# A three-layer block on one core: last chunk's taps on two engines, scores between taps, transposes by pairs of heads, low part and variance moved

## The chip, the cores and the metric

The kernel runs on one core of a Trainium2 chip. The metric is the device time of one launch in microseconds; three runs took 1165.66, 1166.23 and 1166.40 us, median 1166.23. The engines are named as in the profile: TensorE (PE, its weight loads PEld), VectorE (DVE), ScalarE (ACT), GpSimd (POOL) and SyncE (SP), which issues nearly all DMAs.

## The reference

Input x has 256 tokens of 1024 features in float32. Two layers of a first kind are followed by one of a second kind. Cut to what matters here:

```python
# layers 0 and 1: attention over chosen keys beside a gated recurrence, then a gated FFN
h = rmsnorm(x, norm_mix[l]); proj = h @ w_in[l]          # q, k, v, index, recurrence, gates
y_attn = dsa_attention(q, k, v, qi, ki, wi)              # softmax over the 64 keys of the highest index score
y_hgrn = rmsnorm(hgrn2_chunked(q_h, k_in, v_h, log_f)) * silu(hg)
x = x + (sigmoid(ga) * (y_attn @ w_proj_attn[l]) + sigmoid(gb) * (y_hgrn @ w_proj_hgrn[l])) @ w_out[l]
g, u = split(rmsnorm(x, norm_ffn[l]) @ w_ffn_in[l]); x = x + (silu(g) * u) @ w_ffn_out[l]

# third layer: attention with forgetting beside a causal depthwise convolution
attn = fox_attention(q, k, v, log_f)                     # 8 heads of 64, two blocks of 128 queries
u = conv_val * sigmoid(conv_gate)
u = causal_depthwise_conv(u, conv_w, conv_b)             # 31 taps, 512 channels
u = silu(layer_norm(u, conv_ln_g, conv_ln_b))            # mean and variance over the 512 channels
y = concatenate([attn, u]) @ w_o
x = x + g1 * rms_norm(y, mix_post_g); h = rms_norm(x, ffn_pre_g) * (1 + sc2) + sh2
x = x + g2 * rms_norm(swiglu_ffn(h), ffn_post_g)
```

## The kernel before

All activations lie in SBUF with features on the 128 partitions and 256 tokens along the free axis, a chunk being 128 features. Weights stream through in units of at most 128x2048 elements. SP loads each into one of six raw buffers; ACT rounds it to a high part (w_hi, all of ACT stands under L1066), DVE subtracts to get the low part (w_lo, L1609), and TensorE forms three products, high by high, high by low and low by high. Both parts have three buffers, so a unit is split up to three units ahead, once TensorE has finished the unit that held the buffer (unit_done). The order of work is written out by hand, engine by engine: `stream(n)` on TensorE does the next n units, `tick` and `split_ahead` on ACT and DVE split one more, and semaphores (an `Event` each) tie the engines. Parts that several engines share are written as generators: each `next(first)` or `next(second)` takes the attention of the first or second 128 queries one step further, `next(taps)` the last chunk of the convolution.

Attention on TensorE (`attend`, L722): scores for eight heads, then, when ACT's exponentials are done (event a_ex, one for all heads of a query tile), transposes of the probabilities (8 for the first tile, 16 for the second) into four banks that ACT copies out, the products with v, and four transposes of the result, of which ACT makes the high part and DVE the low part (ya_lo, event a_lo). In layers 0 and 1 the recurrence's first products (L958) wait for a_lo of the second tile. DVE makes that low part at L2016, after the decayed queries (L2013), the first block products and a reversed identity.

The convolution of the third layer has four chunks of 128 channels. DVE does chunks 0 to 2 tap by tap (`conv`, L2180), each tap adding one shifted product to an accumulator (conv_acc); over two chunks the operations alternate, over one each waits for the one before. The last chunk is on TensorE (`last_chunk`, L788): 31 matmuls of 256 columns, each with a diagonal of that tap's weights that ACT has made (`diagonals`, L1512), eight per step of the generator; ACT copies the sum and adds the bias (L1569). DVE then folds the four chunks (L2245 to L2250, event c_fold), TensorE sums over the channels (L1041), ACT scales the mean, DVE centres (L2255), ACT squares, DVE folds the squares (c_fold2), TensorE sums them (the variance, L1046), and ACT makes the factor (Ln, Exp), silu and the high parts, and then eight diagonals of gains (`diagonal_gains`), which `gain_rows(0)` (L802) needs. The output projection is four units (L540 to L542 with ya_hi, then conv_out_hi); `gain_rows(0)` stands behind the second, `gain_rows(1)` behind the fourth. Then rows are normed token by token (`mixer_out`, L1185) and transposed back (L825), and the feed-forward's first unit (`high_parts_first`, L830) starts with the high parts alone.

## Time and profile before

| | us |
|---|---|
| median of three runs | 1166.23 |
| lowest, highest | 1165.66, 1166.40 |
| the profiled execution | 1165.65 |
| its span | 1163.9 |
| TensorE busy | 1128.3 (97%) |
| VectorE busy | 857.0 (74%) |
| ScalarE busy | 628.4 (54%) |
| chain that ended last | PE 73%, DVE 17%, ACT 7%, issue 2%, DMA 1% |

The first layer fills the span up to about 420 us, the second up to about 832, the third the rest. Inside the third, the attention and the convolution lie between 896 and 938, the output projection between 937.6 and 961.3. Times in the rows are microseconds from the span's start. A row of the timeline may hold several like instructions (x8); its second number then runs from the first one's start to the last one's end. A matmul's time includes a tail of some 0.2 us that overlaps the next one, so the pace is read from starts. fp32 operands make two records for each tap's matmul. In brackets stands how long the engine was idle before the group, and what released it. Some records of TensorE are missing.

### The profile page before, as it was taken

What the parts mean: (1) busy time and instruction counts of PE and PEld (TensorE: products, weight loads), DVE (VectorE), ACT (ScalarE), POOL (GpSimd) and SP (SyncE); (2) the same over time, 40 slices, a digit from 0 to 9 for tenths busy, and PEclk for the clock granted to TensorE, in tenths of its full rate; (3) what the DMA queues carried; (4) which work ended last, traced back from release to release, by engine and by line L of the source; (5) the groups of instructions that cost most, each with busy time, mean ns of one, the idle gap of its engine ahead of it and who ended that gap; (6) DMA issues with size and microseconds to landing.
All of it is one profiled execution on the core that took longest, in us unless ns stands there. A gap on an engine that the chain in (4) does not pass through costs nothing.

```text
span 1163.9 us, 20299 instructions
## 1 busy us (share of the span) xinstructions
PE 1128.3 (97%) x8518; PEld 1081.5 (93%) x8518; DVE 857.0 (74%) x1348; ACT 628.4 (54%) x802; POOL 0.2 (0%) x4
## 2 busy tenths in 40 slices
PE   6999999999999999999999999999999998999997
PEld 5899899999999998898999999999998888999997
DVE  7896676777889878975767778898689857445544
ACT  6676366464443466673574644344578586434333
POOL 0000000000000000000000000000000000000000
PEclk9999999999999999999999999999999999999999
DMA  9645443756879555554336668796544044565520
GB/s 345 205 145 184 140 136 120 249 185 227 278 250 311 177 166 171 164 184 140 117 113 227 204 205 281 243 322 208 172 140 169 21 155 143 190 192 188 181 73 37
DMA packets 174027, 214.09 MB, mean 184 GB/s; under 512 B 3696, under 2 KB 155632, under 8 KB 173936
## 3 DMA queue, kind: packets, MB, share of 16 engines
q1 hardware_dynamic: 173248, 212.14, 55.6%
q8 instruction: 67, 1.10, 0.4%
q10 hardware_dynamic: 688, 0.66, 0.2%
q14 instruction: 24, 0.20, 0.1%
HBM read 211.74 MB, written 1.05 MB: 183 GB/s over the span
## 4 chain that ended last, share of the span: by engine, by line
PE 73%; DVE 17%; ACT 7%; issue 2%; DMA 1%; DVEq 0%; ACTq 0%
PE stream L540 15%; PE stream L542 15%; PE stream L541 15%; DVE w_lo L1609 7%; PE steps L540 5%; PE steps L541 5%; PE steps L542 5%; ACT w_hi L1066 3%; ACT probs L1066 2%; DVE conv_acc L2190 2%; PE stream L798 1%; PE steps L974 1%; PE steps L777 1%; DVE probs L1801 1%; PE stream L624 1%
## 5 line engine op out<-in xcount | busy, mean ns | idle before, releaser
L1609 DVE TENSOR_TENSOR w_lo<-raw,w_hi 128x2048 fp32r<-128x2048 f32 (+2 forms) x178 | 401.6, 2266 | 187.0 <-ACT w_hi L1066 186.2
L1066 ACT ACTIVATE w_hi<-raw 128x2048 fp32r<-128x2048 f32 (+2 forms) x178 | 336.2, 1892 | 298.1 <-PE stream L542 258.4
L540 PE MATMUL stream<-h_hi,w_hi 128*128 128x256 f32 x1592 | 455.4, 286 | 3.2 <-DVE w_lo L1609 2.8
L541 PE MATMUL stream<-h_lo,w_hi 128*128 128x256 f32 x1592 | 450.4, 283 | 0.0
L542 PE MATMUL stream<-h_hi,w_lo 128*128 128x256 f32 x1592 | 450.3, 283 | 0.0
L540 PEld LDWEIGHTS stream<-h_hi,w_hi 128*128 128x128 f32 x1592 | 305.3, 192 | 7.2 <-DVE w_lo L1609 4.9
L541 PEld LDWEIGHTS stream<-h_lo,w_hi 128*128 128x128 f32 x1592 | 305.4, 192 | 1.4 <-issue 1.0
L542 PEld LDWEIGHTS stream<-h_hi,w_lo 128*128 128x128 f32 x1592 | 305.3, 192 | 0.0
L540 PE MATMUL steps<-gu_hi,w_hi 128*128 128x256 f32 x352 | 100.0, 284 | 0.2 <-DVE gu_lo L1912 0.2
L541 PE MATMUL steps<-gu_lo,w_hi 128*128 128x256 f32 x352 | 99.6, 283 | 0.0
L542 PE MATMUL steps<-gu_hi,w_lo 128*128 128x256 f32 x352 | 99.6, 283 | 0.0
L1880 DVE SCALAR_TENSOR_TENSOR ada_sum<-ada_raw,c_act,ada_sum 128x256 f32<-128x256 f32 x168 | 81.5, 485 | 6.0
L1066 ACT ACTIVATE gu_hi<-gu 128x512 fp32r<-128x512 f32 x33 | 20.9, 632 | 101.6 <-DVE gu L1908 101.6
L540 PEld LDWEIGHTS steps<-gu_hi,w_hi 128*128 128x128 f32 x352 | 67.5, 192 | 0.6 <-issue 0.4
L541 PEld LDWEIGHTS steps<-gu_lo,w_hi 128*128 128x128 f32 x352 | 67.5, 192 | 0.0
L542 PEld LDWEIGHTS steps<-gu_hi,w_lo 128*128 128x128 f32 x352 | 67.5, 192 | 0.0
L624 PE MATMUL stream<-w_hi,h_hi 128*128 128x512 f32 (+1 forms) x152 | 59.5, 391 | 1.4 <-DVE w_lo L1609 1.4
L626 PE MATMUL stream<-w_lo,h_hi 128*128 128x512 f32 (+1 forms) x152 | 58.1, 382 | 0.0
L625 PE MATMUL stream<-w_hi,h_lo 128*128 128x512 f32 (+1 forms) x152 | 57.9, 381 | 0.0
L1912 DVE TENSOR_TENSOR gu_lo<-gu,gu_hi 128x512 fp32r<-128x512 f32 x33 | 22.9, 693 | 23.1 <-ACT gu_hi L1066 23.1
L2190 DVE SCALAR_TENSOR_TENSOR conv_acc<-conv_in,params,conv_acc 128x256 f32<-128x256 f32 x90 | 38.9, 481 | 1.0
L540 PE MATMUL stream<-x_gained_hi,w_hi 128*128 128x256 f32 x128 | 36.8, 287 | 1.0 <-DVE x_gained_lo L1663 1.0
(370 smaller groups left out, 1641.9 us busy)
## 6 DMA issues: line engine op xcount, KB each, us to landing
raw<-in_w_ffn_in SPq DMA_DIRECT2D x66, 1024.0 KB, 5.5
raw<-in_w_in SPq DMA_DIRECT2D x54, 1024.0 KB, 5.3
raw<-in_w_ffn_out SPq DMA_DIRECT2D x33, 1024.0 KB, 5.1
ada_raw<-in_ada_w SPq DMA_DIRECT2D x24, 1024.0 KB, 6.4
raw<-in_w_out SPq DMA_DIRECT2D x8, 1024.0 KB, 5.1
raw<-in_w_proj_attn SPq DMA_DIRECT2D x8, 512.0 KB, 3.5
raw<-in_w_proj_hgrn SPq DMA_DIRECT2D x8, 512.0 KB, 4.5
raw<-in_w_o SPq DMA_DIRECT2D x4, 1024.0 KB, 5.2
```

The costliest lines, as they stand in the source:

```text
L540: pe.matmul(dst, w_h, x_h, start=start, stop=False, skip_group_check=True)
L541: pe.matmul(dst, w_h, x_l, start=False, stop=False, skip_group_check=True)
L542: return pe.matmul(dst, w_l, x_h, start=False, stop=stop, skip_group_check=True)
L624: pe.matmul(dst, h_h[:, k0 + k, ts], hi[:, k, :], start=k0 + k == 0, stop=False)
L625: pe.matmul(dst, h_l[:, k0 + k, ts], hi[:, k, :], start=False, stop=False)
L626: mm = pe.matmul(dst, h_h[:, k0 + k, ts], lo[:, k, :], start=False, stop=k0 + k == KC - 1)
L777: mm = pe.matmul(pv[:, DH * h:DH * h + DH], prT[:, h, s, :], v[:, s, DH * h:DH * h + DH], start=s == 0, stop=s == qt)
L1066: return act.activation(out_, in_, func, **kw)
L1609: tt(wl[m % SPL][:, 0:n], raw[m % RAW][:, 0:n], wh[m % SPL][:, 0:n].bitcast(F32), ALU.subtract)\
L1880: ins = stt(acc, w[:, k, :], cact[:, k:k + 1], acc, ALU.mult, ALU.add)
L1912: tt(gu_l[i % 2].rearrange("p c t -> p (c t)"), gu, gu_h[i % 2].rearrange("p c t -> p (c t)").bitcast(F32), ALU.subtract).then_inc(*lane.m ...
L2190: ins = stt(cv[:, c, :], src, w, cv[:, c, :], ALU.mult, ALU.add)
```

## The change

Seven edits. (1) The last chunk has 23 taps on TensorE; the other eight are on DVE, alternating with the last eight of chunk 2, the first of them with the bias. DVE adds TensorE's sum to them (c_tap, one operation); ACT's copy and eight of its diagonals go. (2) TensorE's taps come in portions of 4, 4 and 15 instead of 8, 8, 8 and 7, with the second tile's scores behind the second portion, and DVE takes these scores ahead of taps 22 and on. (3) In all layers a_ex counts pairs of heads, and the transposes wait pair by pair. (4) In layers 0 and 1 the low part of the second tile stands ahead of the decayed queries. (5) The variance's matmul stands behind the first unit of the output projection, and the fold of the squares behind all of the attention's last steps on DVE; the mean's matmul comes after the products with v. (6) The first square of the updated rows (`x_squares(0)`) comes after the second row factor. (7) In the feed-forward's first unit the first two feature chunks are released one by one.

TensorE, third layer, from the second half of the scores to the projection; q_and_pick and k_and_cum are queries and keys with the decay, conv_diagonal the taps, probs the probabilities, h_norm_third the folded convolution, scratch its squares. Before:

```order
L736 MATMUL steps<-k_and_cum,q_and_pick 128x256 [waits ya_lo_set]
L736 MATMUL steps<-k_and_cum,q_and_pick 128x256 x3
L798 MATMUL stream<-conv_in,conv_diagonal_155 128x256 [waits diagonals_set]
...
L798 MATMUL stream<-conv_in,conv_diagonal_169 128x256
L746 MATMUL steps<-consts,probs 128x128 [waits probs_set]
L746 MATMUL steps<-consts,probs 128x128 x15
L1041 MATMUL stream<-h_norm_third,ones 128x256 [waits conv_folded]
L757 MATMUL steps<-v,probsT 128x64 [waits probsT_set]
...
L767 MATMUL steps<-consts,y_tm 128x128 [waits second_y_scaled]
...
L1046 MATMUL stream<-scratch,ones 128x256 [waits conv_squares_folded]
L767 MATMUL stream<-consts,y_tm 128x128 [waits second_y_scaled,evac_by_act]
...
L540 MATMUL steps<-w_hi_55,ya_hi 128x512 [waits ya_lo_set,second_ya_lo_set,evac_by_act,split_lo]
```

And now (L801 is the taps, L1047 the mean, L1053 the variance, L811 the gain rows):

```order
L738 MATMUL steps<-k_and_cum,q_and_pick 128x256 [waits ya_lo_set]
L738 MATMUL steps<-k_and_cum,q_and_pick 128x256 x3
L801 MATMUL stream<-conv_in,conv_diagonal_147 128x256 [waits diagonals_set]
...
L801 MATMUL stream<-conv_in,conv_diagonal_161 128x256
L749 MATMUL steps<-consts,probs 128x128 [waits probs_set]
L749 MATMUL steps<-consts,probs 128x128 x3
...
L760 MATMUL steps<-v,probsT 128x64 [waits probsT_set]
...
L1047 MATMUL stream<-h_norm_third,ones 128x256 [waits conv_folded]
L770 MATMUL steps<-consts,y_tm 128x128 [waits second_y_scaled]
...
L770 MATMUL stream<-consts,y_tm 128x128 [waits second_y_scaled,evac_by_act]
...
L542 MATMUL steps<-w_hi_55,ya_hi 128x512 [waits ya_lo_set,second_ya_lo_set,evac_by_act,split_lo]
...
L1053 MATMUL stream<-scratch,ones 128x256 [waits conv_squares_folded]
```

The scores moved ahead of the last fifteen taps, there are eight taps fewer, the transposes wait four times, the mean's matmul went behind the products with v, and the variance's matmul from between the last transposes to behind the first unit.

VectorE, third layer, from the first tile's low part to the mean's fold and centring. Before:

```order
L1835 TENSOR_TENSOR ya_lo<-steps,ya_hi 128x4x128 [waits ya_hi_set]
L2190 SCALAR_TENSOR_TENSOR conv_acc<-conv_in,params,conv_acc 128x256 [waits dve_lane] x4
L1801 ISA probs,row_max<-steps,consts 128x256 [waits logits]
...
L1807 TENSOR_SCALAR row_max<-row_max 128x8 [waits dve_lane]
L2190 SCALAR_TENSOR_TENSOR conv_acc<-conv_in,params,conv_acc 128x256 [waits dve_lane] x5
L1609 TENSOR_TENSOR w_lo_58<-raw_52,w_hi_55 128x2048 [waits unit_done,split_hi]
L2245 TENSOR_TENSOR h_norm_third<-conv_acc 128x256 [waits split_lo]
L2247 TENSOR_TENSOR h_norm_third<-h_norm_third,conv_acc 128x256 [waits dve_lane]
L2250 TENSOR_TENSOR h_norm_third<-h_norm_third,conv_acc 128x256 [waits last_chunk_set,dve_lane]
L1609 TENSOR_TENSOR w_lo_59<-raw_53,w_hi_56 128x2048 [waits unit_done,split_hi]
L2255 TENSOR_TENSOR conv_acc<-conv_acc,rstd 128x1024 [waits conv_mean]
```

And now:

```order
L1843 TENSOR_TENSOR ya_lo<-steps,ya_hi 128x4x128 [waits ya_hi_set]
L1809 ISA probs,row_max<-steps,consts 128x256 [waits logits]
...
L1815 TENSOR_SCALAR row_max<-row_max 128x8 [waits dve_lane]
L2199 SCALAR_TENSOR_TENSOR conv_acc<-conv_in,params,conv_acc 128x256 [waits dve_lane] x2
L2196 TENSOR_SCALAR conv_acc<-conv_in,params 128x256
L2199 SCALAR_TENSOR_TENSOR conv_acc<-conv_in,params,conv_acc 128x256 [waits dve_lane] x14
L1617 TENSOR_TENSOR w_lo_58<-raw_52,w_hi_55 128x2048 [waits unit_done,split_hi]
L2255 TENSOR_TENSOR h_norm_third<-conv_acc 128x256 [waits split_lo]
...
L2260 TENSOR_TENSOR conv_acc<-stream,conv_acc 128x256 [waits last_chunk_summed,dve_lane]
L2262 TENSOR_TENSOR h_norm_third<-h_norm_third,conv_acc 128x256 [waits dve_lane]
L1617 TENSOR_TENSOR w_lo_59<-raw_53,w_hi_56 128x2048 [waits unit_done,split_hi]
L2267 TENSOR_TENSOR conv_acc<-conv_acc,rstd 128x1024 [waits conv_mean]
```

The scores come directly behind ya_lo; behind them stand 17 taps' operations where there were five, and four additions where there were three.

VectorE, first layer, between the second tile's result and the recurrence. Before:

```order
L1609 TENSOR_TENSOR w_lo_59<-raw_50,w_hi_56 128x2048 [waits unit_done,split_hi]
L2013 TENSOR_TENSOR hgrn_q_decayed<-hgrn_q,scratch 128x512 [waits hgrn_q_set]
L2013 TENSOR_TENSOR hgrn_q_decayed<-hgrn_q,scratch 128x512
L1845 TENSOR_TENSOR block_forget_99<-scratch 128x512
L2015 TENSOR_TENSOR reversed_ident<-consts,ones 128x128
L1835 TENSOR_TENSOR ya_lo<-steps,ya_hi 128x4x128 [waits ya_hi_set]
```

And now:

```order
L1617 TENSOR_TENSOR w_lo_59<-raw_50,w_hi_56 128x2048 [waits unit_done,split_hi]
L1843 TENSOR_TENSOR ya_lo<-steps,ya_hi 128x4x128 [waits ya_hi_set,hgrn_q_set]
L2022 TENSOR_TENSOR hgrn_q_decayed<-hgrn_q,scratch 128x512 x2
L1853 TENSOR_TENSOR block_forget_99<-scratch 128x512
L2024 TENSOR_TENSOR reversed_ident<-consts,ones 128x128
L1617 TENSOR_TENSOR w_lo_60<-raw_51,w_hi_57 128x2048 [waits unit_done,split_hi]
```

ya_lo moved up over the two products, the block product and the reversed identity.

The diff, less renumbering and declarations:

```diff
@@ -739,9 +741,10 @@
                 if n % 2:
                     mm.then_inc(a_lg.sem, 1)
             yield
-            pe.wait_ge(*a_ex.at(b, qt))
             n_t = 0
             for h in range(H):
+                if h % 2 == 0:
+                    pe.wait_ge(*a_ex.at(b, 4 * qt + h // 2))
                 for s in range(qt + 1):
                     mm = pe.transpose(B[n_t // 4][:, P * (n_t % 4):P * (n_t % 4) + P], pr[:, h, P * s:P * s + P], ident)
                     n_t += 1
@@ -790,12 +793,12 @@
             for e, c in BANKS[UOUT[2] + 3][1]:
                 pe.wait_ge(evac[e], c)
             pe.wait_ge(*evacuated(unit(2, "val1")))
-            for j in range(CONV_K):
+            for j in range(CONV_PE):
+                if j in (4, 8):
+                    yield
                 if j % 8 == 0:
-                    if j:
-                        yield
                     pe.wait_ge(*c_diag.at(0, j // 8))
-                mm = pe.matmul(conv_bank[:, 0:T], diag[j], upad[:, 3, j:j + T], start=j == 0, stop=j == CONV_K - 1)
+                mm = pe.matmul(conv_bank[:, 0:T], diag[j], upad[:, 3, j:j + T], start=j == 0, stop=j == CONV_PE - 1)
             mm.then_inc(c_tap.sem, 1)
             yield
 
@@ -838,8 +841,11 @@
             lo = wl[m % SPL].rearrange("p (k n) -> p k n", k=KC)
             for j in range(4):
                 pairs = [(n, k) for n in range(2) for k in (2 * j, 2 * j + 1)]
-                pe.wait_ge(*n_hi.at(NTH_NORM[5], j))
-                for n, k in pairs:
+                if j:
+                    pe.wait_ge(*n_hi.at(NTH_NORM[5], j))
+                for k, n in ((k, n) for k in (2 * j, 2 * j + 1) for n in range(2)):
+                    if j == 0 and n == 0:
+                        pe.wait_ge(*(n_hi.at(NTH_NORM[5], 0) if k else h_first_hi.at(0)))
                     out, ws = bank(m)[:, T * n:T * n + T], (slice(None), k, slice(P * n, P * n + P))
                     pe.matmul(out, hi[ws], hh[:, k, :], start=k == 0 and n == 0, stop=False, skip_group_check=True)
                     pe.matmul(out, lo[ws], hh[:, k, :], start=False, stop=False, skip_group_check=True)
@@ -1035,18 +1041,18 @@
         next(taps)
         next(second)
         next(taps)
-        next(taps)
+        next(second)
         next(second)
         pe.wait_ge(*c_fold.at(0))
         mm = pe.matmul(conv_bank[:, T:2 * T], ones, hn2[:, 0, :], start=True, stop=True)
         mm.then_inc(c_ms.sem, 1)
         next(second)
         next(second)
+        stream(1)
         pe.wait_ge(*c_fold2.at(0))
         mm = pe.matmul(conv_bank[:, 0:T], ones, scr[:, 0, :], start=True, stop=True)
         mm.then_inc(c_var.sem, 1)
-        next(second)
-        stream(2)
+        stream(1)
         gain_rows(0)
         stream(2)
         gain_rows(1)
@@ -1188,10 +1194,9 @@
             out_squares(1, p_part.at(0, 1))
             out_factor(0)
             out_squares(2, p_part.at(0, 2))
-            x_squares(0)
             out_squares(3, (unit_done, UOUT[2] + 4))
             out_factor(1)
-            for j in range(1, 4):
+            for j in range(4):
                 x_squares(j)
             act.wait_ge(*x_ms2.at(0))
             f(rs_x, rest_x, ACT.Ln, scale=1.0 / D, bias=eps).then_inc(*lane.step())
@@ -1208,7 +1213,13 @@
                           bias=mod[:, 3, k:k + 1]).then_inc(*lane.step())
                     act.wait_ge(*lane.last)
                 else:
+                    if j == 0:
+                        act.wait_ge(*h_first.at(0))
+                        f(hh[:, 0, :], hn2[:, 0, :], ACT.Copy).then_inc(*lane.mark(h_first_hi))
                     act.wait_ge(*n_hn.at(NTH_NORM[5], j if j < 2 else 2))
+                    if j == 0:
+                        f(hh[:, 1, :], hn2[:, 1, :], ACT.Copy).then_inc(*lane.mark(n_hi))
+                        continue
                 f(hh[:, 2 * j:2 * j + 2, :], hn2[:, 2 * j:2 * j + 2, :], ACT.Copy).then_inc(*lane.mark(n_hi))
             rows_in(1)
 
@@ -1228,7 +1239,7 @@
                 scale = qsc[:, H * qt + h:H * qt + h + 1] if b < 2 else SCALE
                 ins = f(pr[:, h, 0:n_s], pr[:, h, 0:n_s], ACT.Exp, scale=scale, bias=mx[:, qt, h:h + 1],
                         accum_out=den[:, qt, h:h + 1])
-                if h == H - 1:
+                if h % 2:
                     ins.then_inc(*lane.mark(a_ex))
                 else:
                     ins.then_inc(*lane.step())
@@ -1561,12 +1572,9 @@
             f(v[:, :, UC * j:UC * j + UC], b2(here()), ACT.Copy).then_inc(*emptied())
             if j == 0:
                 next(first)
-                diagonals(3)
             split_ahead()
         next(first)
         next(second)
-        act.wait_ge(*c_tap.at(0))
-        f(cv[:, 3, :], conv_bank[:, 0:T], ACT.Identity, bias=pc("conv_b", 3)).then_inc(*lane.mark(c_pe))
         next(second)
         act.wait_ge(*gains_set.at(1))
         act.wait_ge(*c_ms.at(0))
@@ -2008,13 +2016,14 @@
             next(second)
             tick()
             dve.wait_ge(*q_act.at(b, 1))
+            next(second)
             for g in range(2):
                 gs = slice(2 * g, 2 * g + 2)
                 tt(qp[:, gs, :], hq[:, gs, :], scr[:, gs, :], ALU.mult).then_inc(*(lane.mark(r_m) if g else lane.step()))
             longer_blocks(0)
             tt(flip, ident[:, ::-1], ones, ALU.mult).then_inc(*lane.mark(flip_set))
-            next(second)
             tick()
+            dve.wait_ge(*flip_set.at(b))
             for t in range(NT):
                 dve.wait_ge(*r_lv.at(b, t))
                 tt(AT[:, :, t, :], A[t].rearrange("p (c q) -> p c q", c=RH),
@@ -2183,7 +2192,7 @@
                 for c in chunks:
                     o = COLS["conv_w"][0] + CONV_K * c + j
                     w, src = par[:, o:o + 1], upad[:, c, j:j + T]
-                    if j == 0:
+                    if j == (0 if c < 3 else CONV_PE):
                         ts_(cv[:, c, :], src, w, pc("conv_b", c), ALU.mult, ALU.add).then_inc(*lane.step())
                     else:
                         dve.wait_ge(lane.sem, lane.count + 1 - len(chunks))
@@ -2236,9 +2245,10 @@
         next(first)
         conv(range(18, 22), (2,))
         next(first)
-        conv(range(22, 26), (2,))
         next(second)
-        conv(range(26, CONV_K), (2,))
+        conv(range(22, CONV_PE), (2,))
+        dve.wait_ge(*lane.last)
+        conv(range(CONV_PE, CONV_K), (2, 3))
         step()
         split_ahead()
         dve.wait_ge(*lane.last)
@@ -2246,20 +2256,21 @@
         dve.wait_ge(*lane.last)
         tt(hn2[:, 0, :], hn2[:, 0, :], cv[:, 2, :], ALU.add).then_inc(*lane.step())
         dve.wait_ge(*lane.last)
-        dve.wait_ge(*c_pe.at(0))
+        dve.wait_ge(*c_tap.at(0))
+        tt(cv[:, 3, :], conv_bank[:, 0:T], cv[:, 3, :], ALU.add).then_inc(*lane.step())
+        dve.wait_ge(*lane.last)
         tt(hn2[:, 0, :], hn2[:, 0, :], cv[:, 3, :], ALU.add).then_inc(*lane.mark(c_fold))
         step()
         split_ahead()
         step()
         dve.wait_ge(*c_mu.at(0))
         tt(cv, cv, rs.unsqueeze(1).broadcast_to([P, 4, T]), ALU.subtract).then_inc(*lane.mark(c_cen))
-        next(second)
+        for _ in range(3):
+            next(second)
         dve.wait_ge(*c_sq.at(0))
         tt(scr[:, 0:2, :], scr[:, 0:2, :], scr[:, 2:4, :], ALU.add).then_inc(*lane.step())
         dve.wait_ge(*lane.last)
         tt(scr[:, 0, :], scr[:, 0, :], scr[:, 1, :], ALU.add).then_inc(*lane.mark(c_fold2))
-        next(second)
-        next(second)
         split_ahead()
         dve.wait_ge(*c_rs.at(0))
         for c in range(4):
```

## Rows read from the trace of the kernel before

**Rows 1.** The page: busy times, share of the span and instructions.
```profile
PE 1128.3 (97%) x8518; PEld 1081.5 (93%) x8518; DVE 857.0 (74%) x1348; ACT 628.4 (54%) x802; POOL 0.2 (0%) x4
```

**Rows 2.** Timeline of TensorE: start us, us, instruction group, idle time before and its releaser.
```profile
80.49 1.09 PE L746 MATMUL steps<-consts,probs 128*128 128x128 f32 x8 [1.04 <-ACT probs L1066]
...
81.34 0.36 PE L540 MATMUL stream<-h_hi,w_hi 128*128 128x256 f32 x1
...
110.28 1.97 PE L746 MATMUL steps<-consts,probs 128*128 128x128 f32 x16 [1.15 <-ACT probs L1066]
...
134.16 2.02 PE L958 MATMUL steps<-hgrn_q,hgrn_k 128*128 128x128 f32 x16 [1.16 <-DVE ya_lo L1835]
...
904.25 1.09 PE L746 MATMUL steps<-consts,probs 128*128 128x128 f32 x8 [0.70 <-ACT probs L1066]
...
936.87 0.70 PE L1046 MATMUL stream<-scratch,ones 128*128 128x256 f32 x2 [0.78 <-DVE scratch L2260]
...
967.49 3.15 PE L825 MATMUL steps<-consts,x_tm_normed 128*128 128x128 f32 x16 [4.22 <-ACT x_tm_normed L1066]
```

**Rows 3.** Timeline of ACT around the second tile's exponentials.
```profile
108.88 0.19 ACT L1066 ACTIVATION_READ_ACCUMULATOR probs<-probs,row_max,qk_sumsq 128x1 f32 x1
```

**Rows 4.** Timeline of DVE ahead of the recurrence, first layer.
```profile
131.33 1.29 DVE L2013 TENSOR_TENSOR hgrn_q_decayed<-hgrn_q,scratch 128x512 f32<-128x512 f32 x2
...
133.34 0.68 DVE L1835 TENSOR_TENSOR ya_lo<-steps,ya_hi 128x512 fp32r<-128x512 f32 x1
```

**Rows 5.** Timeline of TensorE, third layer, last chunk's taps to the first gain rows.
```profile
921.80 1.89 PE L736 MATMUL steps<-k_and_cum,q_and_pick 72*128 72x256 f32 x8
...
923.52 6.64 PE L798 MATMUL stream<-conv_in,conv_diagonal 128*128 128x256 f32 x30
...
930.00 1.91 PE L746 MATMUL steps<-consts,probs 128*128 128x128 f32 x16
...
935.70 0.39 PE L767 MATMUL steps<-consts,y_tm 128*128 128x128 f32 x2
...
937.63 0.47 PE L540 MATMUL steps<-w_hi,ya_hi 128*128 128x512 f32 x1
...
948.63 1.95 PE L808 MATMUL stream<-gain_diagonal,ones 128*128 128x128 f32 x16
```

**Rows 6.** Timeline of DVE, third layer, convolution and its mean.
```profile
882.87 3.25 DVE L2190 SCALAR_TENSOR_TENSOR conv_acc<-conv_in,params,conv_acc 128x256 f32<-128x256 f32 x8
...
915.27 2.04 DVE L2190 SCALAR_TENSOR_TENSOR conv_acc<-conv_in,params,conv_acc 128x256 f32<-128x256 f32 x4
...
924.62 2.56 DVE L2190 SCALAR_TENSOR_TENSOR conv_acc<-conv_in,params,conv_acc 128x256 f32<-128x256 f32 x5
...
927.09 2.28 DVE L1609 TENSOR_TENSOR w_lo<-raw,w_hi 128x2048 fp32r<-128x2048 f32 x1
...
930.78 0.43 DVE L2250 TENSOR_TENSOR h_norm_third<-h_norm_third,conv_acc 128x256 f32<-128x256 f32 x1 [0.49 <-ACT conv_acc L1066]
...
933.33 1.22 DVE L2255 TENSOR_TENSOR conv_acc<-conv_acc,rstd 128x1024 f32<-128x1024 f32 x1
```

**Rows 7.** Timeline of ACT, third layer, behind the variance.
```profile
939.52 0.48 ACT L1066 ACTIVATE rstd<-stream,consts 128x256 f32<-128x256 f32 x1
...
945.18 2.44 ACT L1066 ACTIVATE gain_diagonal<-consts,gain 128x128 f32<-128x128 f32 x8
...
961.45 0.63 ACT L1066 ACTIVATE h_norm_third<-xT 128x512 f32<-128x512 f32 x1 [0.24 <-DVE xT L2282]
```

**Rows 8.** Stretch: busy time and instructions of each engine, granted clock (PEclk), DMA share, GB/s.
```profile
967.50:972.00 4.50, 4.50 (x26) 4.50 (x27) 3.75 (x9) 2.97 (x6) 0.00 (x0) 0.62 0.00 0
```

**Rows 9.** Timeline of TensorE at the start of the first layer.
```profile
21.43 0.50 PE L624 MATMUL stream<-w_hi,h_hi 128*128 128x512 f32 x1 [1.43 <-DVE w_lo L1609]
...
22.78 0.63 PE L626 MATMUL stream<-w_lo,h_hi 128*128 128x512 f32 x1
...
23.20 0.63 PE L624 MATMUL stream<-w_hi,h_hi 128*128 128x512 f32 x1
```

More of the change, by code:

```diff
@@ L39 @@
 CONV_K = 31
+CONV_PE = 23
 SCALE = DH ** -0.5
@@ L269, in build @@
     cv = at("conv_acc", [P, 4, T], F32, 188)
-    diag = [at(f"conv_diagonal{j}", [P, P], F32, (194, 155, 148, 124)[j // 8] + 0.5 * (j % 8)) for j in range(CONV_K)]
+    diag = [at(f"conv_diagonal{j}", [P, P], F32, (194, 155, 148)[j // 8] + 0.5 * (j % 8)) for j in range(CONV_PE)]
     yc_h = at("conv_out_hi", [P, 4, T], F32R, 148)
@@ L401, in build @@
     a_lg, a_mx, a_ex, a_pt, a_pte, a_pv, a_y, a_yt, a_hi, a_lo = (Event(n, k) for n, k in (
-        ("logits", 8), ("row_max_set", 2), ("probs_set", 2), ("probs_transposed", 6), ("probsT_set", 6),
+        ("logits", 8), ("row_max_set", 2), ("probs_set", 8), ("probs_transposed", 6), ("probsT_set", 6),
         ("attended", 2), ("y_scaled", 2), ("y_transposed", 2), ("ya_hi_set", 2), ("ya_lo_set", 2)))
@@ L420, in build @@
     evac["gu"] = f_gu.sem
-    c_diag, c_tap, c_pe = Event("diagonals_set", 4), Event("last_chunk_summed"), Event("last_chunk_set")
+    c_diag, c_tap = Event("diagonals_set", 3), Event("last_chunk_summed")
+    h_first, h_first_hi = Event("third_first_normed"), Event("third_first_hi")
     c_fold2 = Event("conv_squares_folded")
@@ L1512, in diagonals @@
         def diagonals(n):
-            for j in range(8 * n, min(8 * n + 8, CONV_K)):
+            for j in range(8 * n, min(8 * n + 8, CONV_PE)):
                 o = COLS["conv_w"][0] + CONV_K * 3 + j
                 ins = f(diag[j], ident, ACT.Copy, scale=par[:, o:o + 1])
-                ins.then_inc(*(lane.mark(c_diag) if j in (7, 15, 23, CONV_K - 1) else lane.step()))
+                ins.then_inc(*(lane.mark(c_diag) if j in (7, 15, CONV_PE - 1) else lane.step()))
         tick()
@@ L1808, in attend @@
             yield
-            dve.wait_ge(*a_ex.at(b, qt))
+            dve.wait_ge(*a_ex.at(b, 4 * qt + 3))
             dve.reciprocal(den[:, qt, :], den[:, qt, :]).then_inc(*lane.step())
@@ L2305, in affine @@
                           ALU.mult, ALU.add)
-                ins.then_inc(*(lane.mark(n_hn) if k % 2 else lane.step()))
+                ins.then_inc(*(lane.mark(n_hn) if k % 2 else lane.step() if j else lane.mark(h_first)))
         def low(j):
```

## Prediction

> **What bounds the kernel now.** I read the page's busy rows first, then TensorE's timeline for its pauses, then the timelines of the three engines around the places that the change touches, and last the granted clock. TensorE is busy for 1128.3 of 1163.9 us [rows 1], so time is won only by taking TensorE's work away or by closing its pauses, and it is lost wherever a new pause opens. The reader is to see in [rows 2] that the first layer has three pauses at places of the change: 1.04 and 1.15 us before the transposes of the probabilities and 1.16 us before the recurrence's first products. The second layer repeats all three to the hundredth. The third has 0.70 us before its first transposes and 0.78 us before the variance's matmul; its large one, 4.22 us, lies behind the output projection, where TensorE has nothing to do until the rows are normed [rows 2].
>
> **Transposes by pairs of heads, layers 0 and 1.** Before, the first transpose waits for the last of eight exponentials and starts at 80.49; the next projection starts 0.85 us later, 0.107 a transpose [rows 2]. Released by pairs, the first six fit into the pause of 1.04, and at 80.49 only two are left: 0.85 - 0.21 = 0.64 us saved. With 256 keys there are sixteen, some 1.75 us (1.97 with the last one's tail). There the third pair's exponentials end at 109.07 [rows 3], before TensorE is free at 109.13 (110.28 less 1.15), so twelve are ready and take until 110.43, by when the last pair is too: all 1.15 us of the pause go. The three extra waits hold nothing back: queued behind them is the next projection, whose weights were split before. Bounds: 0.4 to 0.7, and 0.9 to 1.15, a switch between waits at a tenth at most.
>
> **Low part earlier.** DVE's subtraction ya_lo runs at 133.34, behind two products (1.29 [rows 4]), a block product and the flip, and TensorE waits for it until 134.16 [rows 2]. Moved ahead of them it runs at about 131.4 and is done at 132.0, while TensorE's stream ends at 133.0 (134.16 less 1.16). Late next is the q product, which now stands behind: done at about 133.3, wanted only after the next half unit, four microseconds later. Gain 1.16, between 0.9 and 1.3.
> Per layer 0.64 + 1.15 + 1.16 = 2.95, for two layers 5.9 us (4.4 to 6.3).
>
> **Third layer, up to the output projection.** The pair rule saves 0.64 before v's second half. What follows is set down in the time of the trace before. Fifteen taps take 6.48 us, from 923.52 to 930.00 [rows 5]: 0.432 a tap, so eight fewer are 3.5 us. Counted back from the scores at 921.80 over two times eight taps and four transposes (0.44), the taps began at 914.4; now at 913.8. Four taps, four transposes, four taps: the second half of the scores starts at 917.7 instead of 921.80 and takes 1.72, fifteen taps 6.48, until 925.9, sixteen transposes until 927.65 (all exponentials are done by 924.6, so pairs gain nothing here), the products with v 3.5, until 931.2. Before, that point was 935.70 [rows 5]: TensorE is 4.5 us early.
> DVE is not. Its row maxima end 2.8 us behind the scores' start, as before (924.62 [rows 6]), at 920.5. Then come tap 22 of chunk 2 (0.51: four of a single chain take 2.04 [rows 6]) and sixteen operations in two chains. Eight of two chains take 3.25 with the tail, 0.397 each [rows 6]; sixteen 6.35, until 927.4. Before, the convolution ended at 927.09 [rows 6]. Then w_lo (2.2) and four additions instead of three; before, the third waited for ACT's copy of the sum until 930.78 [rows 6], which goes, and the new one (0.46) takes its place: the fold is done at 931.5, before at 931.1. Behind it stand w_lo (to 933.7), the centring (1.15, to 934.85, before from 933.33 [rows 6]), the reciprocal and y's first half, at 935.45. So TensorE does the mean's matmul at 931.5 and then pauses from 931.95 to 935.5 for y's first half: a new pause of 3.5 us in place of the taps. ACT's high and DVE's low part of that half take 1.3 us more; the projection's first unit starts at 936.85, before at 937.63 [rows 5]. Of taps, pair rule and the pause of 0.78 together, 4.9 us, only 0.8 are left.
>
> The Trainium skill speaks against the 0.397: "VectorE: DVE Perf Modes", section "The DRAIN you can't avoid", says that each operation waits for the pipeline to empty and that a semaphore after each adds nothing. By it two chains would run at the pace of one, 16 x 0.51 = 8.2 us, and the sum would be 1.8 us worse. [Rows 6] show 0.397 against 0.51 in this kernel, so the rows decide.
>
> **The variance, moved.** Its matmul now follows the first unit (two units take from 937.63 to 948.63 [rows 5], 5.5 us each), at 942.35. ACT's logarithm needs it: it started at 939.52 and will at 943.05. From there ACT's order is fixed: Ln, Exp, a table load, four silus and copies, eight gain diagonals, which start at 945.18 and end at 947.6 [rows 7], 8.0 us behind the logarithm. They will be ready at 951.1. TensorE wants them (L808) after the second unit, at 948.2; before it came at 948.63 [rows 5], 1.0 us after they were ready. That is a second new pause, of 2.9 us, and L808 starts 2.5 us later than before. Set against it: ahead of the first unit the variance would have waited for its squares until 938.3, 1.4 us.
> From L808 on the lateness stays, since ACT has behind the diagonals one queue (w_hi, rows, second diagonals, two w_hi, squares), 2.7 us late. x_squares(0) (0.63 [rows 7]) no longer stands ahead of the fourth square, which saves 0.4. The transposes of the normed rows start 2.3 us later than at 967.49.
>
> **The clock.** After the pause of 4.22 us the granted clock is 0.62 over 967.5 to 972 [rows 2, 8], (1 - 0.62) x 2 x 4.5 = 3.4 us at the lower level. At 21.43, after a pause of 1.43 us with two short transposes ahead, records of 512 columns last 0.63 us and start every 0.42 [rows 9], while those of the projection start every 0.229 (48 in 11.0 us [rows 5]): 1.2 instead of 2.4 GHz. Both new pauses are twice that at 21.43. If each is followed by such a stretch, of which about 3.1 us lie in work, it loses 47% there: 1.5 us behind the first, and 1.2 behind the second, where L808's short matmuls lose less. Bounds 0 and 1.7 each. I take both.
> The Trainium skill ("TensorE: Matmul & The Clock Gate", section "HAM oscillation — how this bites in real kernels") has a rule of the kind: waits between bursts of matmuls bring the clock down, and the next burst starts slow. By it the trace agrees. It speaks against this change; without it the sum would be 2.7 us better.
>
> **High parts in the third layer's first unit.** Half a pair is copied alone. Before, TensorE comes out of its transposes, which run in the slow stretch [rows 8], later than the whole pair is copied; gain 0 (0.5 where the clock is up).
> **Nothing for** the eight diagonals (2.15 us of ACT, hidden by its wait for v's second half) and for SP, whose queue holds the same DMAs in the same order.
>
> **Sum.** -5.9 + 2.3 (which holds the 0.64) + 1.5 + 1.2 = -0.9 us. The profiled execution took 1165.65, so 1164.75; the median of the runs is 0.58 above it: 1165.3 us.
>
> **The rivals.**
> A, my forecast: both pauses open and the clock falls after both, 1165.3 (1163.8 to 1166.8). Chance 0.48.
> B, the pauses open but the clock holds, or falls after one only. For it: pauses of 1.0 to 1.4 us with work around them leave it at 1.00; against it the two falls above. -5.9 + 2.3 = -3.6: 1162.6, with one fall 1163.9. Chance 0.25.
> C, the second pause does not open, because L808 does not wait for the variance's chain on ACT: -5.9 - 0.8 = -6.7, 1159.5. Against it the fixed order on ACT and the slack of 1.0 us. Chance 0.12.
> D, slower: the 5.9 us of layers 0 and 1 are given back inside the layer, because TensorE, early now, finds the recurrence's decayed keys not ready: these come from DVE, whose w_lo ahead of them waits for ACT and not for what was moved. The third layer then stands alone, +5.0: 1171.2. It decides for slower from 3.2 us given back (2.3 + 0.9). Against it: every level's products have a half unit of cover, some 2.9 us, against one microsecond of DVE's work. Chance 0.15, 0.11 of it beyond the bound.
>
> A difference under 0.2% (2.3 us) can't be told from none. Below 1163.9 lie all of C, most of B (0.22) and the low end of A (0.06): faster 0.40, slower 0.11, same 0.49. Range 1161.0 to 1168.0; it leaves out C and the far half of D.
>
> **What would show it.** Right: in layers 0 and 1 the pauses before the transposes shrink to some 0.5 and 0, and the one before the recurrence goes; in the third layer over 3 us of pause behind the mean's matmul, about 3 us before L808's successor, released by ACT's gain_diagonal, and a lower granted clock behind both. Wrong: a fold on DVE far later than 2.2 us after the convolution plus four additions, diagonals that are ready at the old distance from the projection's start, or a clock of 1.00 from 930 to 960.

## The result, and the profile after

The changed kernel takes 1167.37 us (median of 15 runs, 1165.27 to 1169.02), the kernel before 1165.66 us beside it: ratio 1.0015, 95% interval 1.0008 to 1.0022. It is slower by 0.15%, under the bound of 0.2%, yet clear of zero; the forecast was 1165.3, 0.9 us faster than the 1166.23 known then. The time lies in the range of 1161.0 to 1168.0, and the sign is wrong.

The profiled execution of the changed kernel is the fastest of its 15: 1165.27 us, span 1162.9. Its page, busy times:

```profile
PE 1128.8 (97%) x8502; PEld 1081.1 (93%) x8502; DVE 859.3 (74%) x1357; ACT 625.7 (54%) x794; POOL 0.2 (0%) x4
```

Fewer taps, but TensorE is 0.5 us busier than in [rows 1]: its matmuls ran longer. Its timeline at the places of [rows 2, 5]:

```profile
79.94 0.44 PE L749 MATMUL steps<-consts,probs 128*128 128x128 f32 x2 [0.38 <-ACT probs L1072]
...
130.96 1.95 PE L964 MATMUL steps<-hgrn_q,hgrn_k 128*128 128x128 f32 x16
...
889.74 2.02 PE L738 MATMUL steps<-k_and_cum,q_and_pick 72*128 72x128 f32 x16 [1.39 <-ACT k_and_cum L1072]
...
925.42 0.70 PE L1047 MATMUL stream<-h_norm_third,ones 128*128 128x256 f32 x2
929.33 0.44 PE L770 MATMUL steps<-consts,y_tm 128*128 128x128 f32 x2 [3.21 <-DVE y_tm L1826]
...
946.25 3.26 PE L811 MATMUL stream<-gain_diagonal,ones 128*128 128x128 f32 x16 [2.72 <-ACT gain_diagonal L1072]
...
966.54 2.90 PE L828 MATMUL steps<-consts,x_tm_normed 128*128 128x128 f32 x16 [3.93 <-ACT x_tm_normed L1072]
```

The pause ahead of the first transposes is 0.38 where [rows 2] have 1.04, and the recurrence starts at 130.96 with no pause. The third layer's first scores (L738) start at 889.74; in the trace of before they start at 895.78:

```profile
895.78 2.02 PE L736 MATMUL steps<-k_and_cum,q_and_pick 72*128 72x128 f32 x16 [1.39 <-ACT k_and_cum L1066]
```

So 6.04 us are won by there. Of them 0.95 are left at the transposes of the normed rows (966.54 against 967.49). Between lie the two new pauses, 3.21 us ahead of y's transposes and 2.72 us ahead of the gain rows. DVE and ACT, timeline of the changed kernel, show what is late:

```profile
915.70 5.62 DVE L2199 SCALAR_TENSOR_TENSOR conv_acc<-conv_in,params,conv_acc 128x256 f32<-128x256 f32 x14
...
925.28 2.29 DVE L1617 TENSOR_TENSOR w_lo<-raw,w_hi 128x2048 fp32r<-128x2048 f32 x1
927.48 1.22 DVE L2267 TENSOR_TENSOR conv_acc<-conv_acc,rstd 128x1024 f32<-128x1024 f32 x1
...
928.85 0.75 DVE L1826 TENSOR_TENSOR y_tm<-steps,row_sum 128x256 f32<-128x256 f32 x2
```

```profile
938.12 0.48 ACT L1072 ACTIVATE rstd<-stream,consts 128x256 f32<-128x256 f32 x1 [6.03 <-PE stream L1053]
...
943.77 2.43 ACT L1072 ACTIVATE gain_diagonal<-consts,gain 128x128 f32<-128x128 f32 x8
```

Behind the fold (its last addition ends at 925.37) y waits on DVE for a w_lo and the centring (3.4 us). The diagonals end 8.1 us behind the logarithm, as in [rows 7], but the logarithm now waits 6.03 us for a matmul that stands behind the first unit.

### The profile page after: what moved, and what is told of

It reads as the page before. It is cut to its first block, busy times and chain, and to the rows that moved or that the text cites. A ratio compares the mean times of both kernels' runs of the same rounds, so it can differ in the third digit from the quotient of the medians.

```text
span 1162.9 us, 20273 instructions
## 1 busy us (share of the span) xinstructions
PE 1128.8 (97%) x8502; PEld 1081.1 (93%) x8502; DVE 859.3 (74%) x1357; ACT 625.7 (54%) x794; POOL 0.2 (0%) x4
## 4 chain that ended last, share of the span: by engine, by line
PE 74%; DVE 18%; ACT 5%; issue 2%; DMA 1%; SPq 0%; DVEq 0%; ACTq 0%
PE stream L542 15%; PE stream L543 15%; PE stream L544 15%; DVE w_lo L1617 7%; PE steps L542 6%; PE steps L543 5%; PE steps L544 5%; ACT w_hi L1072 2%; DVE conv_acc L2199 2%; PE stream L626 1%; PE stream L628 1%; PE stream L627 1%; DVE score L1789 1%; PE steps L980 1%; DVE top L1787 1%
```

## The experiments

Each kernel ran beside the kernel before, which took 1165.66 us in the median of the 15 runs beside the changed kernel, 1165.75 beside a1 to a4, 1165.72 beside b1 to b4 and 1165.84 beside c1 to c4; each ratio is to the one beside it. "Third" is, in the profiled execution, the time from the third layer's first scores to the transposes of the normed rows; "outside" is the median of a run's time less its span. A profile is of one execution, and not always of a typical one: those of after, a2, a4, b2 and c3 are of the fastest of their runs, those of a3, b1 and c1 of the slowest. In a3, b1, b3, c1, c2 and c4 "third" also holds a fall of the clock at 892 to 896 us, behind the pause of 1.39 us ahead of the scores, which the trace of before does not have; from the scores to the first tile's products with v these take 17.4 to 17.5 us against 16.2 in a4, 1.2 us more.

| kernel | median us (runs) | ratio, 95% interval | clock, median | third, us | outside |
|---|---|---|---|---|---|
| before | 1165.75 (27) | 1 | 0.996 | 71.71 | 1.81 |
| changed | 1167.37 (15) | 1.0008 to 1.0022 | 0.991 | 76.80 | 2.37 |
| a1, changed again | 1167.22 (11) | 1.0004 to 1.0022 | 0.991 | 77.71 | 2.38 |
| a2, pairs and low part | 1160.38 (5) | 0.9939 to 0.9966 | 0.996 | 71.07 | 1.80 |
| a3, variance back | 1165.01 (11) | 0.9983 to 1.0000 | 0.992 | 76.55 | 2.25 |
| a4, fillers | 1163.47 (11) | 0.9970 to 0.9987 | 0.997 | 74.10 | 2.31 |
| b1, y ahead of centring | 1162.08 (6) | 0.9955 to 0.9979 | 0.995 | 76.02 | 2.36 |
| b2, diagonals ahead | 1163.65 (11) | 0.9976 to 0.9993 | 0.992 | 73.19 | 2.35 |
| b3, both orders | 1161.55 (5) | 0.9947 to 0.9972 | 0.994 | 71.83 | 2.39 |
| b4, a2 with edits 6, 7 | 1159.28 (5) | 0.9933 to 0.9958 | 0.996 | 70.77 | 1.78 |
| c1, a2 with edit 5 | 1167.61 (11) | 1.0010 to 1.0027 | 0.995 | 80.44 | 1.80 |
| c2, a2 with edits 1, 2 | 1165.72 (11) | 0.9987 to 1.0005 | 0.990 | 76.22 | 2.17 |
| c3, w_lo moved | 1159.86 (5) | 0.9940 to 0.9965 | 0.996 | 71.34 | 1.77 |
| c4, c3 with filler | 1160.31 (5) | 0.9937 to 0.9965 | 0.996 | 72.61 | 1.81 |

**a1, the changed kernel again.** No edit.

> The changed kernel once more, for a profile of a typical execution. Theory T: in the trace of after the pauses are where they were foreseen and are worth -3.6 us without the clock (-5.9 in layers 0 and 1, +2.3 in the third layer); what was mis-sized is the clock's part, for the profiled execution has four stretches of 3.4 us at the lower level (granted clock 0.994) where the median one has six (0.991), each costing about 1.1 us. So 1167.4 us, clock 0.991, and the profile, if it is of such an execution, shows the added stretches between 925 and 966 us, behind the two new pauses. Rival R: the lost time lies in longer waits (fold on VectorE, diagonals on ScalarE), and the pauses of the trace are over 3.5 and 3.2 us.

Measured: 1167.22 us, and this profile is of a typical execution (1167.26 us, span 1164.9). TensorE's timeline, then windows (from : to in us, length, TensorE busy, granted clock, DMA share, GB/s). Windows of the profiled execution of after follow, with the busy times of PE, PEld, DVE, ACT and POOL; the second is half a microsecond longer.

```profile
890.10 2.02 PE L738 MATMUL steps<-k_and_cum,q_and_pick 72*128 72x128 f32 x16 [1.39 <-ACT k_and_cum L1072]
...
929.69 0.69 PE L770 MATMUL steps<-consts,y_tm 128*128 128x128 f32 x2 [3.21 <-DVE y_tm L1826]
...
947.52 2.57 PE L811 MATMUL stream<-gain_diagonal,ones 128*128 128x128 f32 x16 [2.72 <-ACT gain_diagonal L1072]
...
967.81 3.43 PE L828 MATMUL steps<-consts,x_tm_normed 128*128 128x128 f32 x15 [3.94 <-ACT x_tm_normed L1072]
```

```profile
928.00:938.00 10.00, 7.72 (x25) 0.66 0.53 168
...
946.50:954.00 7.50, 6.48 (x30) 0.77 0.14 43
964.00:974.00 10.00, 6.19 (x34) 0.66 0.01 2
```

```profile
928.00:938.00 10.00, 8.25 (x31) 6.37 (x32) 5.64 (x9) 3.11 (x4) 0.00 (x0) 0.83 0.55 179
...
946.00:954.00 8.00, 7.75 (x35) 6.92 (x36) 2.29 (x1) 6.93 (x13) 0.00 (x0) 0.79 0.32 97
```

The pauses are the same to the hundredth (3.21, 2.72, and 3.94 against 3.93). The clock is not: a clock of 0.66 over 10 us is 6.8 us at the lower level behind the first pause, against 3.4 us in the execution shown before. Behind the last pause it is the same, 0.66 from 964 to 974 us where after has 0.83. Rival R's longer waits are not there. The spans differ by 2.0 us: 0.9 behind the first pause, 0.7 behind the last, and 0.4 that a1 is already late at the third layer's first scores (890.10 against 889.74). Over both sets of runs time goes with the clock: executions at 0.994 took 1165.3 to 1166.0 us, those at 0.989 1168.7 to 1169.0.

**a4, fillers in the pauses.** The same waits, with TensorE kept at work in them:

```diff
         mm.then_inc(c_ms.sem, 1)
+        for _ in range(7):
+            pe.matmul(A[3][:, 0:T], ones, ident.unsqueeze(1).broadcast_to([P, 2, P]), start=True, stop=True)
...
         stream(1)
+        for _ in range(6):
+            pe.matmul(row_bank[0][0][:, 0:T], ones, ident.unsqueeze(1).broadcast_to([P, 2, P]), start=True, stop=True)
         gain_rows(0)
```

> The changed kernel with idle work for TensorE: seven more matmuls of 256 columns, whose sums nobody reads, behind the mean's matmul, and six behind the second unit, each 0.43 us, 3.0 and 2.6 us in all, inside the pauses of 3.2 and 2.7 us. Theory T (the loss is the clock's fall behind the two pauses): nothing waits longer, the stretches at the lower level behind both pauses go, the granted clock is back near 0.997, and the time is 1165.7 - 3.6 = 1162.1 us (1161 to 1163.5). Rival R (waits or transfers, not the clock): 1167 or more, as the changed kernel or slower.

Measured: 1163.47 us, 3.8 under the changed kernel at a clock of 0.997. Timeline and windows:

```profile
889.92 2.02 PE L738 MATMUL steps<-k_and_cum,q_and_pick 72*128 72x128 f32 x16 [1.39 <-ACT k_and_cum L1076]
...
926.14 3.19 PE L1050 MATMUL steps<-consts,ones 128*128 128x256 f32 x14
929.51 0.44 PE L770 MATMUL steps<-consts,y_tm 128*128 128x128 f32 x2 [0.19 <-DVE y_tm L1830]
...
945.31 2.05 PE L811 MATMUL stream<-gain_diagonal,ones 128*128 128x128 f32 x16
...
964.02 1.94 PE L828 MATMUL steps<-consts,x_tm_normed 128*128 128x128 f32 x16 [3.94 <-ACT x_tm_normed L1076]
```

```profile
926.00:945.00 19.00, 18.18 (x82) 1.00 0.46 154
945.00:960.00 15.00, 14.87 (x81) 1.00 0.43 141
```

This is the fastest of the 11 executions (1162.10 us). The clock stays at 1.00, behind the last pause too, and "third" is 74.10: the waits alone cost 2.39 us against before (forecast 2.3), and the clock took 3.6 us of a1's 77.71. From y's transposes to the gain rows it is 15.80 us here, 16.92 in after and 17.83 in a1; from the gain rows to the last transposes 18.71, and 20.29 in both others. So the clock costs 1.1 us behind the first pause in after and 2.0 in a1, and 1.6 behind the second in both. That is theory T, and R falls. The median is 1.4 us above T's value: 0.5 of it is time outside the span; the rest fits executions at 0.995 to 0.997.

**a2, pairs of heads and low part alone; a3, the variance's matmul back ahead of the first unit.** a2 is edits 3 and 4 on the kernel before (in the diff above), a3 is:

```diff
-        stream(1)
         pe.wait_ge(*c_fold2.at(0))
...
-        stream(1)
+        stream(2)
         gain_rows(0)
```

> The kernel before with two edits alone: transposes released by pairs of heads in all layers, and the low part of the second tile moved up in layers 0 and 1. Theory T: -2.95 us per layer for two layers as predicted, nothing more in the third (VectorE bounds it there), clock as before 0.997: 1165.7 - 5.9 = 1159.8 us (1159 to 1160.5). Rival D (the gain of layers 0 and 1 is given back inside the layer, or later): 1163 or above. Rival R (the slowdown of the whole change is of these edits, by the clock): 1165 or above with a clock of 0.995 or less.

> The changed kernel with the variance's matmul back ahead of the output projection's first unit. Theory T: TensorE waits 1.6 us for the fold of the squares ahead of the first unit, which starts 2.1 us later than in after; in return the eight gain diagonals are ready when TensorE comes to them, so the pause of 2.7 us ahead of the gain rows goes and they start some 1.9 us earlier than in after. Without the clock -5.5 us against before; with two stretches at the lower level behind the first pause (2.2 us) 1162.4 us (1161 to 1164), and none behind the second unit. Rival R (the variance's place does not matter, something later on ScalarE bounds the rows): 1166 to 1168 as after.

a2 took 1160.38 us, 5.4 less and in T's range; its profile, of the fastest run, reaches the third layer's scores at 889.68, 6.1 us earlier than before, and in it "third" is 0.64 shorter too, the pair rule's gain ahead of v's second half, which the expectation had left out. Rival D, gain given back, falls. a3 took 1165.01, 2.6 over T's value, outside its range and below R's. TensorE's timeline of a3:

```profile
931.49 0.69 PE L770 MATMUL steps<-consts,y_tm 128*128 128x128 f32 x2 [3.21 <-DVE y_tm L1825]
931.97 0.63 PE L770 MATMUL stream<-consts,y_tm 128*128 128x128 f32 x2
934.59 1.22 PE L1052 MATMUL stream<-scratch,ones 128*128 128x256 f32 x2 [1.99 <-DVE scratch L2272]
```

The second pause is gone, as T has it. But two pauses stand in a row here, 3.21 and 1.99 us, with little between, and behind them the clock is 0.63 from 928 to 942 us, 10.4 us at the lower level where T had 6.8. This is the slowest of the 11 executions; the median clock of all is 0.992, as low as the changed kernel's within 0.001. How the 2.6 us divide is not shown.

**b1, b2, b3: the two pauses closed by order.** b1 on DVE (and ACT's high part ahead of its squares), b2 on ACT, b3 both:

```diff
         step()
-        split_ahead()
-        step()
+        next(second)
+        next(second)
         dve.wait_ge(*c_mu.at(0))
         tt(cv, cv, rs.unsqueeze(1).broadcast_to([P, 4, T]), ALU.subtract).then_inc(*lane.mark(c_cen))
-        for _ in range(3):
-            next(second)
+        next(second)
+        split_ahead()
+        step()
```

```diff
+        diagonal_gains(0)
         rstd(rs, conv_bank[:, 0:T], 512, c_var.at(0), c_rs)
...
-        diagonal_gains(0)
         tick()
```

> The changed kernel, but the second tile's last steps do not queue behind the mean on VectorE and ScalarE: the scaling of y stands directly behind the fold, then centring, then its low part, then w_lo; ScalarE makes its high part ahead of the squares. Theory T: the first pause (3.2 us behind the mean's matmul) goes nearly whole, the projection starts some 2.6 us earlier than in after (about 928.2), and the clock no longer falls there (two stretches, some 2.2 us in a typical execution); the second pause stays at 2.7 us, since the diagonals still come 8.0 us behind the logarithm, with one or two stretches behind it. 1167.3 - 2.6 - 2.2 = 1162.5 us (1161.5 to 1164.5). Rival R (what is late moves to the fold of the squares or to the second pause and takes it back): second pause over 4 us and 1165.5 or more.

> The changed kernel, but ScalarE makes the first eight gain diagonals (2.4 us) ahead of the variance's logarithm, in the five microseconds in which it waits. Theory T: the second pause goes (2.7 us) with the stretch at the lower level behind it (1.1 us); the first pause and its stretches stay. 1167.3 - 2.7 - 1.1 = 1163.5 us (1162 to 1165). Rival R: the rows' squares or the third large pause ahead of the transposes grow by as much, 1166 or more.

> Both orders together on the changed kernel. Theory T: no pause over 0.7 us from the mean's matmul to the second gain rows, clock at 0.997, 1167.3 - 2.6 - 2.7 - 3.3 = 1158.7 us (1157.5 to 1160.5), the fastest of all so far. Rival R (gains of the two do not add, ScalarE or VectorE bound the projection): 1161 or more.

b1 took 1162.08 us and b2 1163.65, both within T's ranges. Of b1's mechanism one part does not hold: in its profile, of the slowest of six runs, 1.51 us of the first pause stay and 3.4 us at the lower level follow them, where T had none. In b2 the second pause and its low clock are gone, as T has it, and the last pause grew from 3.93 to 4.42 us. b3 took 1161.55, outside T's range and in rival R's: the gains do not add. TensorE's timeline of b3, then windows:

```profile
929.89 0.77 PE L542 MATMUL steps<-w_hi,ya_hi 128*128 128x512 f32 x1 [1.51 <-DVE ya_lo L1832]
...
942.83 1.95 PE L811 MATMUL stream<-gain_diagonal,ones 128*128 128x128 f32 x16
...
961.89 3.65 PE L828 MATMUL steps<-consts,x_tm_normed 128*128 128x128 f32 x16 [4.42 <-ACT x_tm_normed L1072]
```

```profile
892.00:896.00 4.00, 4.00 (x23) 0.57 0.45 131
928.00:936.00 8.00, 6.49 (x22) 0.79 0.52 177
```

The gain rows no longer wait. Ahead of the projection 1.51 us stay, since the centring stands ahead of ya_lo, and the clock falls behind them (0.79 from 928 to 936 us, 3.4 us at the lower level); the last pause grew to 4.42. With both repairs "third" is 71.83, before it was 71.71, but that is not because the waits gave nothing. The fall behind the 1.51 us costs 1.5 us (from the projection's start to the gain rows 12.94 us, against 11.45 from there to the fillers in a4), the one at 892 us 1.2. Without both "third" is 69.1, 5.0 under a4's 74.10, where T had 5.3: the waits went as foreseen, and the clock did not come back. Against b4 below (70.77, no fall of the clock from 890 to 960 us), which has all its taps on TensorE, 69.1 is 1.7 less: the 3.5 us of taps are worth 1.7 in waits. The clock, 0.8 us behind the last pause (from there to the end 197.2 us against b4's 196.4) and 0.6 outside the span take more than that back.

**c1, c2: the two suspects one by one on a2.** c1 is edit 5, c2 edits 1 and 2.

> Pairs of heads and the earlier low part (1160.4 us) with the variance edit alone added: variance's matmul behind the first unit, fold of the squares behind the attention's last steps, mean's matmul behind the products with v. Theory T: the pause of 0.78 us goes, the projection starts 0.5 us earlier, and TensorE waits 2.7 us for the diagonals ahead of the gain rows, with one or two stretches at the lower level behind it: 1160.4 + 2.6 + 1.1 to 2.2 = 1164.5 us (1163.5 to 1165.3). Rival V (the taps alone make the slowdown): 1161 or less.

> Pairs of heads and the earlier low part with the taps edits alone added (23 taps on TensorE, eight on VectorE, portions of 4, 4 and 15). Theory T: a pause of about 3.9 us ahead of the mean's matmul, since VectorE folds at the old time, the projection starts some 0.9 us later, and the clock falls behind the pause for two stretches: 1160.4 + 0.9 + 2.0 = 1163.3 us (1162 to 1164.5). Rival V' (the variance alone makes the slowdown): 1160.5 or less. Time outside the span: 2.3 us here and 1.8 with the variance alone if it comes with the taps, the other way round if with the variance.

c1 took 1167.61 us, 7.2 over a2 and 3.1 over T's value; c2 1165.72, 5.3 over a2 and 2.4 over it. Both are outside T's ranges, and V and V' fall: either part alone slows a2 by more than 5 us. The whole change is 7.0 over a2, so the parts do not add. c1's profile is of the slowest of its 11 runs, c2's of one near the median. Timeline of c1, TensorE and DVE:

```profile
930.43 0.65 PE L1043 MATMUL stream<-h_norm_third,ones 128*128 128x256 f32 x2
933.45 0.69 PE L768 MATMUL steps<-consts,y_tm 128*128 128x128 f32 x2 [2.37 <-DVE y_tm L1820]
```

```profile
931.60 1.22 DVE L2258 TENSOR_TENSOR conv_acc<-conv_acc,rstd 128x1024 f32<-128x1024 f32 x1 [3.02 <-ACT rstd L1068]
```

I had overlooked in edit 5 that the mean's matmul goes behind the products with v: with all taps on TensorE that makes VectorE wait 3.02 us for the mean, and a first pause of 2.37 us opens that T did not have. In the whole change it costs nothing, since there the products are done before the fold. TensorE's timeline of c2:

```profile
927.26 1.22 PE L1042 MATMUL stream<-h_norm_third,ones 128*128 128x256 f32 x2 [3.66 <-DVE h_norm_third L2252]
928.27 6.93 PE L759 MATMUL steps<-v,probsT 128*128 128x64 f32 x32
```

The pause is the one foreseen (3.66). Behind it the products with v take 6.93 us where c1 has 3.68, at a clock of 0.53 from 926 to 936.5: ten microseconds at the lower level, three times what the prediction gave a pause and half again what the expectation gave this one.

**b4, c3, c4: towards a faster kernel.** b4 is a2 with edits 6 and 7; c3 moves one `split_ahead()` on DVE from ahead of the centring to behind ya_lo; c4 puts eight fillers behind `gain_rows(1)`.

> The kernel before with four of the seven edits: pairs of heads, low part earlier, the first square of the updated rows later, and the feed-forward's first chunks released one by one. Theory T: the pause ahead of the transposes of the normed rows falls by 0.3 us (4.2 to 3.9), the released chunks bring 0 where the clock is down and up to 0.5 where it is up: 1160.4 - 0.3 = 1160.1 us (1159.3 to 1160.6). Beside it, the time outside the span, which is 2.4 us in the changed kernel and 1.8 in the kernel before and in that with two edits: if it is 2.3 or more here, one of these two edits brings it (they add a semaphore), if 1.8, it comes with the taps or the variance.

> The fastest so far (pairs, low part, later square, released chunks: 1159.3 us), with one w_lo on VectorE moved from ahead of the centring to behind the attention's last steps. Theory T: the squares are folded before TensorE comes, the pause of 0.78 us ahead of the variance's matmul goes and nothing replaces it: 1159.3 - 0.8 = 1158.5 us (1157.8 to 1159.2), clock 0.997. Rival: w_lo is late for the second unit, 1160 or more.

> The kernel with w_lo behind the squares and with eight more matmuls of 256 columns, whose sums nobody reads (3.5 us), in the pause of 3.9 us ahead of the transposes of the normed rows. Theory T: nothing waits longer, and the stretch of 3.4 us at the lower level behind that pause goes: 1158.5 - 1.2 = 1157.3 us (1156.3 to 1158.2). Rival (that stretch lies under work that ScalarE and VectorE bound, as the released chunks do): 1158.5, no gain.

b4 took 1159.28 us (T 1160.1), the fastest, 0.55% under the kernel before (0.42 to 0.67%); its time outside the span is 1.78, so edits 6 and 7 do not bring the 0.6 us. c3 (1159.86) and c4 (1160.31) gain nothing on it and lie above T's ranges. TensorE's timeline of c3:

```profile
930.12 0.70 PE L1051 MATMUL stream<-scratch,ones 128*128 128x256 f32 x2 [0.48 <-DVE scratch L2269]
...
942.65 2.05 PE L810 MATMUL stream<-gain_diagonal,ones 128*128 128x128 f32 x16 [0.61 <-ACT gain_diagonal L1071]
```

Of the 0.78 us 0.3 go, since the centring now waits for the mean (1.81 us on VectorE), and 0.61 open ahead of the gain rows: two w_lo now stand ahead of the normalization on VectorE, and the diagonals are late. In c4 the filler holds the clock (1.00 from 962 to 967 us, 0.66 in c3 from 961 to 966), and from the transposes to the end it takes 195.8 us against 196.4; with five runs each the median does not show it. The same stretch of the launch takes 195.8 us in a4 (no fall behind a pause of 3.94 us), 196.4 in before and after (3.4 us at the lower level) and 197.1 in a1 (6.8).

## Why the prediction was wrong

For its own execution -0.9 us was forecast and -0.4 measured (1165.27 against 1165.65). There the clock behind the two pauses cost 2.7 us ("third" 76.80 less a4's 74.10), just what the sum had (1.1 and 1.6 for 1.5 and 1.2). But this is the fastest of 15 executions, so the match is luck. What failed is the term of the clock for a typical execution, and with it two terms put at nothing. With a1 against the profile of before, the sum of 1.6 us (1167.26 less 1165.65) is:

| step | forecast | a1 less before |
|---|---|---|
| layers 0 and 1 | -5.9 | -5.7 (after: -6.0) |
| waits in the third layer | +2.3 | +2.4 (a4) |
| clock behind the first new pause | +1.5 | +2.0 |
| clock behind the second | +1.2 | +1.6 |
| clock behind the last pause | 0 | +0.7 |
| outside the span | 0 | +0.6 |

- **Pairs, low part**: right; a2 alone gives -5.4 in the median (-4.0 to -7.1). The pair rule's 0.64 in the third layer is held by the +2.3.
- **Third layer's waits**: right. The pauses were put at 3.5 and 2.9 us and are 3.21 and 2.72. The two-chain pace of 0.397 held: fourteen operations in 5.62 us in after, where four of a single chain take 2.04. By what the Trainium skill says of the pace ("VectorE: DVE Perf Modes", section "The DRAIN you can't avoid") sixteen would have taken 1.8 us longer; this trace does not agree with it.
- **The clock**: "If each is followed by such a stretch, of which about 3.1 us lie in work" is the step that failed. It took the stretch behind the 4.22 us pause and that at 21.43 for the rule. The typical execution a1 has 6.8 us at the lower level behind the first pause and 6.8 behind the last. Over all runs the clock of 0.991 against 0.996 is some 11.7 us more at that level (2 x 0.005 x 1165), where the sum held 6.8. Its upper bound of 1.7 was too low for the first pause (2.0). The Trainium skill ("TensorE: Matmul & The Clock Gate", section "HAM oscillation — how this bites in real kernels") names the mechanism, and a1 against a4 agrees with it: same waits, 3.6 us apart.
- **Outside the span**: 0.57 us more than before, not foreseen. It comes with the taps (c2 2.17, a3 2.25; c1 and b4 1.80 and 1.78). The traces do not show what it is; this stays open.
- **The level**: the forecast set the median of before 0.58 us above its profile, from three runs; 27 runs put it 0.1 above. That moves 1165.3, not the difference of -0.9.
- **Rivals**: B (the clock holds) is refuted by the windows of after, C by the 2.72 us ahead of the gain rows, D by a2. B's argument that pauses of 1.0 to 1.4 us leave the clock at 1.00 holds in the trace of before, but not in six others at the pause of 1.39 us. The time came out slower by A's mechanism, for which the prediction had only D.

Why the clock stays low once or twice as long behind the same pause, or does not fall at all, in executions with pauses alike to the hundredth, is not settled either.

## What to carry to other kernels

Here two new pauses of 5.9 us together on TensorE cost a typical execution 3.6 us more by the clock behind them (2.7 in the fastest). Read the clock of all runs, not of the profiled one, since the profile may be of the luckiest. Before taking work from the busiest engine, ask who is late at the next meeting point: here VectorE was, with its fold and what stands behind it, and 3.5 us less on TensorE mostly made a pause of 3.2. Waits split finer (pairs of heads) or an operation moved ahead of its neighbours gave what had been worked out for them where TensorE was otherwise busy.

## What was not expected of the hardware

- Useless matmuls in a pause pay: 13 of them (5.6 us of TensorE's time) made the kernel 3.8 us faster (a4 against the changed kernel).
- Two pauses close together (a3: 3.21 and 1.99 us) or short matmuls behind one (c2: 3.66 us) came with ten microseconds at the lower level instead of three to seven. Each is one trace, a3's of its slowest run.
- The pause of 1.39 us ahead of the third layer's scores is in all fourteen traces. In eight the clock stays at 1.00 behind it, in six (a3, b1, b3, c1, c2, c4) it falls for 3.4 us, which costs 1.2 us.
- Kernels that differ only in the middle have 1.8 or 2.2 to 2.4 us outside the span. Whether it lies ahead of the first instruction or behind the last, no trace shows.
